# Experts' first product of a 1-core mixture block: weights as the stationary operand, gathered rows moving

## The reference, cut

```python
def swiglu_clamped(h):
    glu = jnp.minimum(h[..., ::2], SWIGLU_LIMIT)
    lin = jnp.clip(h[..., 1::2], -SWIGLU_LIMIT, SWIGLU_LIMIT)
    return glu * jax.nn.sigmoid(SWIGLU_ALPHA * glu) * (lin + 1.0)
...
    xs = xt[slot_tok].reshape(nb, MOE_BLOCK, D)

    def expert_block(args):
        xb, e = args
        hid = xb @ w1[e] + b1[e]
        return swiglu_clamped(hid) @ w2[e] + b2[e]

    ys = lax.map(expert_block, (xs, block_e)).reshape(P, D)
    out = jax.ops.segment_sum(ys.astype(jnp.float32) * slot_w[:, None], slot_tok, num_segments=T)
```

## Time and profile before

| | us |
|---|---|
| median of 3 runs | 3551.31 (3549.64 to 3569.22) |
| profiled execution | 3563.45 |
| its span | 3561.6 |
| mean granted TensorE clock in it | 0.933 |

### The profile page before, as it was taken

One profiled execution on the slowest core, in us unless ns is written; L12 is line 12 of the kernel. 1 busy time (PEld: TensorE's weight loads), 2 busy tenths in 40 slices (PEclk: granted clock), 3 DMA queues, 4 the chain that ended last, 5 costly groups with the idle time before them and its releaser, 6 DMA issues.

```text
span 3561.6 us, 42339 instructions
## 1 busy us (share of the span) xinstructions
PE 3276.9 (92%) x15738; PEld 2693.2 (76%) x15738; DVE 2349.4 (66%) x2341; ACT 1573.6 (44%) x1576; POOL 187.6 (5%) x212
## 2 busy tenths in 40 slices
PE   7967997999999988999999987769999999999995
PEld 6756986877778757878787765658888888888884
DVE  4545336457763556467754437459999999999995
ACT  2142214242223434332223215247777777777772
POOL 0000000000000000000000000001111111111110
PEclk9958978999999989999999996779999999999997
DMA  5200002334443302334433310259999999999993
GB/s 180 86 1 1 1 2 71 105 114 130 144 131 101 95 30 87 99 104 148 142 107 113 100 53 7 89 220 372 377 390 377 389 379 388 378 389 377 389 378 129
DMA packets 118820, 638.42 MB, mean 179 GB/s; under 512 B 13416, under 2 KB 13416, under 8 KB 68784
## 3 DMA queue, kind: packets, MB, share of 16 engines
q1 hardware_dynamic: 98592, 560.52, 42.5%
q0 software_dynamic: 20112, 76.24, 7.1%
HBM read 612.07 MB, written 24.64 MB: 179 GB/s over the span
## 4 chain that ended last, share of the span: by engine, by line
PE 74%; DVE 8%; ACT 1%; issue 1%; DMA 1%; DVEq 0%; SPq 0%; ACTq 0%; POOLq 0%
PE banks L328 25%; PE banks L2657 19%; PE banks L2674 10%; PE banks L1029 7%; PE banks L341 3%; DVE chunk_split L301 1%; PE banks L2651 1%; PE banks L2642 1%; PE banks L2663 1%; PE banks L547 1%; PE banks L570 1%; PE banks L1983 1%; DVE scratch L1127 0%; DVE scratch L389 0%; DVE scratch L1123 0%
## 5 line engine op out<-in xcount | busy, mean ns | idle before, releaser
L328 PE MATMUL banks<-x_scratch,chunk_split 128*128 128x512 f32 x3648 | 846.5, 393 | 36.4 <-DVE x_scratch L315 22.7
L328 PEld LDWEIGHTS banks<-x_scratch,chunk_split 128*128 128x128 f32 x3648 | 686.5, 189 | 190.1 <-issue 47.7
L295 ACT CAST chunk_split<-weight_ring 128x1024 fp32r<-128x1024 f32 x292 | 306.3, 1049 | 957.6 <-PE banks L328 721.0
L2657 PE MATMUL banks<-pair_split,rows 128*128 128x512 f32 x3072 | 709.9, 392 | 0.0
L2657 PEld LDWEIGHTS banks<-pair_split,rows 128*128 128x128 f32 x3072 | 578.6, 188 | 126.5
L301 DVE TENSOR_TENSOR chunk_split<-weight_ring,chunk_split 128x1024 fp32r<-128x1024 f32 x292 | 357.2, 1223 | 211.0 <-ACT chunk_split L295 202.4
L2674 PE MATMUL banks<-pair_split,hidden_t 128*128 128x512 f32 x1536 | 361.4, 394 | 6.1 <-DVE hidden_t L2769 6.1
L2674 PEld LDWEIGHTS banks<-pair_split,hidden_t 128*128 128x128 f32 x1536 | 285.5, 189 | 69.1 <-issue 6.3
L2436 DVE TENSOR_TENSOR pair_split<-mixed,pair_split 128x2048 fp32r<-128x2048 f32 x128 | 293.1, 2291 | 34.4 <-ACT pair_split L2431 34.4
L2436 DVE TENSOR_TENSOR pair_split<-scratch,pair_split 128x2048 fp32r<-128x2048 f32 x128 | 290.4, 2289 | 36.8 <-ACT pair_split L2431 36.8
L2436 DVE TENSOR_TENSOR pair_split<-weight_ring,pair_split 128x2048 fp32r<-128x2048 f32 x128 | 290.3, 2289 | 36.1 <-ACT pair_split L2431 36.1
(11 more groups left out here) (600 smaller groups left out, 3945.9 us busy)
## 6 DMA issues: line engine op xcount, KB each, us to landing
weight_ring<-in_weights SPq DMA_DIRECT2D x292, 512.0 KB, 3.7
mixed<-in_w SPq DMA_DIRECT2D x128, 1024.0 KB, 8.9
weight_ring<-in_w SPq DMA_DIRECT2D x128, 1024.0 KB, 7.8
scratch<-in_w SPq DMA_DIRECT2D x128, 1024.0 KB, 8.6
mixed<-in_w_ada POOLq DMA_DIRECT2D x48, 512.0 KB, 3.8
token_sums<-tables POOLq DMA_DIRECT2D x1, 2560.0 KB, 21.5
residual<-in_x POOLq DMA_DIRECT2D x4, 512.0 KB, 10.4
projected<-in_mem POOLq DMA_DIRECT2D x2, 1024.0 KB, 5.2
```

Source lines behind the costliest of these rows:

```text
L295: act.copy(chunk_split[:, 0, at:at + KB * P], flat(ring[:, n % RING])).then_inc(chunk_hi.sem, 1)
L328: mm = pe.matmul(lin.bank(j), chunk_split[:, a, at + k * P:at + (k + 1) * P], lin.split[b][k][:, 0:lin.tokens], start=(k, a, b) == (0, 0, ...
L2657: mm = pe.matmul(banks[:, n, :], rows[:, a, k, :], pair_split[k % SLOTS][:, b, n * T:(n + 1) * T], start=False, stop=(k, a) == (KB - 1, 1))
```

## The change

In the first product the operands trade places. The stationary operand is now a block of a pair, 128 input features x 128 output features, and the moving one a 128 x 128 block of the gathered rows. Sixteen blocks of each pair go to sixteen 128-column regions of banks 0 to 3, each with the three products, so output features lie on partitions and tokens along the banks. The columns of `w1` and `b1` are put apart on the host (all `glu`, then all `lin`), so banks 0 and 1 hold `glu`, 2 and 3 `lin`. The hidden block is then already in the layout of the second product: `turn_hidden` and its semaphores go, and `hidden_out` reads `lin` in SBUF. The bias has its rows on partitions 0 to 7 in another arrangement and becomes the stationary operand of its matmul, whose contraction is 8 rows. PE has a new wait for `lin_ready` ahead of each first product in the loop, since nothing else now says that the banks have been read.

```diff
-                dve.scalar_tensor_tensor(b1_pick[:, n, :], vec("part").to_broadcast([P, P]), float(32 + n),
+                dve.scalar_tensor_tensor(b1_pick[:, n, :], vec("part").to_broadcast([P, P]), float(4 + n),
...
                     pe.wait_ge(b1_copied, count)
+                    if not isinstance(count, int):
+                        pe.wait_ge(lin_ready, count + (-1))
                     for n in range(4):
-                        mm = pe.matmul(banks[:, n, :], b1_pick[:, n, :], b1_split, start=True, stop=False)
+                        mm = pe.matmul(banks[:, n, :], b1_split[0:8, n * P:(n + 1) * P],
+                                       b1_pick[0:8].rearrange("p n c -> p (n c)"), start=True, stop=False, skip_group_check=True)
                     mm.then_inc(b1_used, 1)
                     for k in range(PAIRS_IN):
                         pe.wait_ge(pair_lo, number + (k + 1))
-                        for a, b in PARTS:
-                            for n in range(4):
-                                mm = pe.matmul(banks[:, n, :], rows[:, a, k, :], pair_split[k % SLOTS][:, b, n * T:(n + 1) * T],
-                                               start=False, stop=(k, a) == (KB - 1, 1))
+                        for m in range(2 * KB):
+                            for a, b in PARTS:
+                                mm = pe.matmul(banks[:, m // 4, (m % 4) * P:(m % 4 + 1) * P],
+                                               pair_split[k % SLOTS][:, b, m * P:(m + 1) * P], rows[:, a, k, :],
+                                               start=False, stop=(k, a) == (KB - 1, 1), skip_group_check=True)
                         mm.then_inc(pair_used, 1)
-
-                def turn_hidden():
...
                 def hidden_out(count):
-                    act.wait_ge(hidden_turned, count)
-                    act.copy(hid_t[:, 0], banks[:, 6:8, :].rearrange("p b (k s) -> p (b k) s", s=P)).then_inc(hidden_hi, 1)
+                    act.wait_ge(hidden_ready, count)
+                    act.copy(hid_t[:, 0], lin.rearrange("p (k s) -> p k s", s=P)).then_inc(hidden_hi, 1)
...
-                    halves = banks[:, 0:4, :].rearrange("p b (f two) -> p b f two", two=2)
-                    dve.tensor_scalar(glu.rearrange("p (b f) -> p b f", b=4), halves[:, :, :, 0], 7.0, None, ALU.min)\
+                    dve.tensor_scalar(glu.rearrange("p (b f) -> p b f", b=2), banks[:, 0:2, :], 7.0, None, ALU.min)\
...
-                    sp.dma_start(b1_rows[32 * part:32 * part + 4, :], src.rearrange("a (n t) -> (a n) t", n=4))\
+                    sp.dma_start(b1_rows[4 * part:4 * part + 4, :].rearrange("q (n p) -> q n p", p=P),
+                                 src.rearrange("a (n q p) -> (a q) n p", n=4, q=4))\
                         .then_inc(b1_landed, 16)
```

More of the change, by code:

```diff
@@ L2400, in program @@
         b1_rows, b1_split = region(SCR_AT + 33 * T, T), rounded_tensor("b1_split", SCR_AT + 34 * T, T)
-        b1_turn, b1_stored, b1_zeroed = sem("b1_turn"), sem("b1_stored"), sem("b1_zeroed")
+        b1_turn, b1_stored = sem("b1_turn"), sem("b1_stored")
         b1_landed, b1_copied, b1_used = sem("b1_landed"), sem("b1_copied"), sem("b1_used")
@@ L2404, in program @@
         glu_ready, lin_ready, silu_out, hidden_ready = sem("glu_ready"), sem("lin_ready"), sem("silu_out"), sem("hidden_ready")
-        hidden_turned, hidden_hi, hidden_lo = sem("hidden_turned"), sem("hidden_hi"), sem("hidden_lo")
+        hidden_hi, hidden_lo = sem("hidden_hi"), sem("hidden_lo")
         y_ready, scattered, row_in_ready, row_out_ready, asked = sem("y_ready"), sem("scattered"), sem("row_in_ready"), sem("row_out_ready"), sem("asked")
@@ L2457, in store_tokens @@
         def store_tokens(pool):
-            pool.memset(b1_rows, 0.0).then_inc(b1_zeroed, 1)
             pool.wait_ge(b1_turn, 2)
@@ L2654, in first_product @@
                         pe.wait_ge(pair_lo, number + (k + 1))
-                        for a, b in PARTS:
-                            for n in range(4):
-                                mm = pe.matmul(banks[:, n, :], rows[:, a, k, :], pair_split[k % SLOTS][:, b, n * T:(n + 1) * T],
-                                               start=False, stop=(k, a) == (KB - 1, 1))
-                        mm.then_inc(pair_used, 1)
-                def turn_hidden():
[L2662 to L2665, removed]
+                        for m in range(2 * KB):
[3 more added lines that the diff above has]
+                                               start=False, stop=(k, a) == (KB - 1, 1), skip_group_check=True)
+                        mm.then_inc(pair_used, 1)
                 def second_product(number):
@@ L2681, in pe @@
                 turn_rows(2)
-                pe.wait_ge(hidden_ready, 1)
-                pe.wait_ge(rows_lo, 2)
-                turn_hidden()
                 last = last_item(pe)
@@ L2691, in pe @@
                     second_product(pair_number(i, PAIRS_IN))
-                    pe.wait_ge(hidden_ready, i + 2)
-                    pe.wait_ge(rows_lo, i + 3)
-                    turn_hidden()
                 pe.wait_ge(hidden_lo, last + 1)
@@ L2757, in hidden @@
                     dve.wait_ge(pair_used, used)
-                    halves = banks[:, 0:4, :].rearrange("p b (f two) -> p b f two", two=2)
-                    dve.tensor_scalar(glu.rearrange("p (b f) -> p b f", b=4), halves[:, :, :, 0], 7.0, None, ALU.min)\
+                    dve.tensor_scalar(glu.rearrange("p (b f) -> p b f", b=2), banks[:, 0:2, :], 7.0, None, ALU.min)\
                        .then_inc(glu_ready, 1)
-                    dve.tensor_scalar(lin.rearrange("p (b f) -> p b f", b=4), halves[:, :, :, 1], 7.0, -7.0, ALU.min, ALU.max)\
+                    dve.tensor_scalar(lin.rearrange("p (b f) -> p b f", b=2), banks[:, 2:4, :], 7.0, -7.0, ALU.min, ALU.max)\
                        .then_inc(lin_ready, 1)
@@ L2768, in hidden_out @@
                     dve.wait_ge(hidden_hi, count)
-                    dve.tensor_tensor(hid_t[:, 1], banks[:, 6:8, :].rearrange("p b (k s) -> p (b k) s", s=P), hid_t[:, 0],
+                    dve.tensor_tensor(hid_t[:, 1], lin.rearrange("p (k s) -> p k s", s=P), hid_t[:, 0],
                                       ALU.subtract).then_inc(hidden_lo, 1)
@@ L2864, in expert_loads @@
             sp.wait_ge(b1_stored, 32)
-            sp.wait_ge(b1_zeroed, 1)
             bias(0, 0)
@@ L3130, in _pack @@
     out["b_router"] = a["b_router_2"].reshape(1, E_N)
-    out["w1"], out["b1"] = a["w1_2"][0].reshape(E_N * KB, P, 2 * D), a["b1_2"][0].reshape(E_N * 4, T)
+    out["w1"] = a["w1_2"][0].reshape(E_N * KB, P, D, 2).transpose(0, 1, 3, 2).reshape(E_N * KB, P, 2 * D)
+    out["b1"] = a["b1_2"][0].reshape(E_N, D, 2).transpose(0, 2, 1).reshape(E_N * 4, T)
     out["w2"] = a["w2_2"][0].reshape(E_N * KB // 2, 2, P, D).transpose(0, 2, 1, 3).reshape(E_N * KB // 2, P, 2 * D)
```

## The result

The changed kernel takes 4790.71 us (median of 4 executions) against 3557.13 us for the kernel before, measured side by side: 1.344 times as long, 95% interval 1.337 to 1.352. The forecast was 4140 us. The sign was right; the size was not: +1234 us where +588 was forecast, less than half. The time lies in the stated range, between the forecast and the 5250 to 5440 us of rival B.

What follows compares the result with a forecast made beforehand. The prediction took PE, busy 92% of the span, to bound the kernel. First product +619, transposes -25, start and tail -6 made +588 us: 4151 on the profiled execution, 4140 against the median; range 4100 to 5500 us.

Steps and rivals of the forecast that it cites:

- rival B: First product: granted clock falls to 0.50 under the short matmuls, 213 ns each; 5250 to 5440 us; chance 0.25.
- The bound and the loads: PE alone sets the item's time; first product's 12,288 stationary loads, four times as many, set the pitch: +619 us.
- The load-record view: First product: summing load records, 12,288 at 188 ns, gives 2310 us, +1608; the prediction rejected it.
- C: First product: short moving operands stream like plain fp32, two records each, 232 ns; 5670 us; chance 0.10.
- E: First product: loads vanish beside the streaming, 57.2 ns a matmul; 3520 us; chance 0.03.
- D: First product: loads hide better, 66 ns pitch, 3630 us, or some 3815 at 81 ns; chance 0.12.
- what lies beside PE: Clamp, rounding, bias DMAs, GpSimd clearing and added wait: priced at nothing; 77 us if the cover failed.
- Rows 8: Trace rows: matmuls on 64 of 128 rows, read as back to back from 446.75; clock 1.00 at 451, 0.50 from 455.
- The pitch: First product: short matmuls 107.5 ns apart from start to start, +619 us; with 120 ns, +772 us.
- The start: First two items: PE's gap shrinks, -7 us; short matmuls at 1.2 GHz until the clock rises, +2 us.
- Rows 7: Trace rows: full 128x128 loads with 128 and 64 columns, 213 to 229 us, clock 0.50, 213 ns each.
- Transposes and tail: Hidden block's transposes go, 0.79 us x 32 = -25 us; wait before the last second product, perhaps -1 us.

Runs made afterwards that it cites:

- the kernel with the raised start: Changed kernel with 128-row bias, plus 24 unused 512-column matmuls ahead of the first two items' first products: 4195.08 us.

## Why the prediction was right or wrong

**The bound and the loads** were right: PE alone sets the item, loads are four times as many, and the pitch is that of a load, not of 128 columns. The load-record view would have given +1608 us for the loads alone; with the clock held, the kernel with the raised start pays +641 in all. Rivals C and E are out by the pitch, and so is D: at a granted clock of 1.00 the matmuls stand 111.8 ns apart, where D had 66. The Trainium skill, page "TensorE: Matmul & The Clock Gate", section "Back-to-back issue gap", has about 81 ns for sustained matmuls of 128 columns; for these fp32r operands it doesn't hold. Its section "LDWEIGHTS (loading the stationary operand)" has the columns over 1.2, which makes an estimate of 106.7 ns, near the measured value at the full clock and half of the 213.5 ns at the lower one.

**The step that failed** is the clock of the first product. The forecast priced all 12,288 short matmuls at the full clock and set rival B, the fall, apart as something for the whole loop; the trace has both, item by item. The sum had no term for what the change does to the four bias matmuls: the part on what lies beside PE speaks only of their DMAs, while the matmuls went from 128 rows to 8. The runs with the bias on 128 rows, left out, moved and doubled show that these tip the clock, where they stand between 512-column matmuls and short ones. Without that the changed kernel takes 4274.71 us instead of 4790.71: 516 us, for 13 items of 39 us and their second products.

**Rival B** had the price of an item's fall, 213 ns a matmul, but its cause only in part. It let the short matmuls bring the clock down because they leave the array idle for half of each load. With 128 columns they did not: behind full-height matmuls they kept 1.00 for 43 us in all 30 items. With 64 columns they did. Rows 8 were also misread. The half-height matmuls do not run back to back until the clock is down; PE first waits 0.67 us for VectorE, and the clock, 1.00 up to that wait, is 0.50 behind it:

```profile
454.48 3.97 PE L1640 MATMUL banks<-projected,scratch 64*128 64x128 f32 x16 [0.67 <-DVE scratch L1728]
```

So they hinted that matmuls on part of the rows do little for the clock, and did not show it. The prediction used them for the short matmuls, which use all rows, and not for the one group in the change that uses 8.

**The pitch was mis-sized** by 4.3 ns: 107.5 taken from the one-column rows, 111.8 measured, inside the bounds of 107.5 and 120. That is 12,288 x 4.3 ns = 53 us, 619 against 671.

**The start** had the right sign for the gap and not for the clock. PE's gap after the first item shrank from 12.01 us to 3.22, -8.8 where -7 was reckoned. But the clock was to rise within a few us of short matmuls, +2 us; it didn't rise at all in the first two items, 2 x 39 = 78 us. Rows 7 had shown just this, 16 us of short matmuls at 0.50. The three terms, 516 for the bias matmuls, 78 for the start and 53 for the pitch, make 647 of the 651 us between 4140 and 4791.

**Transposes and tail.** The 0.79 us a transposed block was right (the 128-row kernel with old operands is 30 us faster than before, for 26 forecast). The 8-row bias took 0.4 us of it back in every item, which no row had shown. The wait before the last second product did not shrink: 6.71 us for 6.06. `lin_ready` never held PE, and no copy came onto the path.

## What to carry to other kernels

Before swapping operands, count stationary loads, not columns: with 64 or 128 moving columns of fp32r data the load set the pace here, 112 ns for each 128x128 block at the full clock, and 256 columns came at 120 ns. Then ask of each stretch what clock it leaves for the next: load-bound matmuls of 128 columns lived on a clock that others had raised, and one microsecond of matmuls on 8 rows at the seam lost it for 80 us in 13 of 30 items. If such matmuls are needed, put them inside the dense stretch, or give them full height with zeros.

## What the runs showed of the hardware that was not expected

- The granted clock has a memory. The same 384 short matmuls, back to back, ran at 1.00 for 43 us or at 0.50 for 82 us, by what was ahead of them. The Trainium skill, page "TensorE: Matmul & The Clock Gate", section "Part 1: The HAM clock gate", says that "the default state is throttled, and activity releases the throttle"; the runs add that a PE with no idle time may not be active enough: 82 us of short matmuls didn't release it. Twenty-four 512-column ones ahead of them did, both times; eight did in one item of two.
- Matmuls on 8 rows count for little in this: 1.1 us of them between the dense and the short matmuls cost 13 of 30 items the full clock, 2.1 us all of them, 2.0 us on 128 rows none in the trace. Rows of zeros were enough for that.
- The number of moving columns counts too: behind the same full-height bias, short matmuls of 128 columns kept the clock in 30 items of 30, those of 64 columns, at the same pitch, in none.
- A load of a 128x128 fp32r block with a short matmul behind it takes 213.5 ns at 1.2 GHz, whether 64 or 128 columns follow (81.96 and 82.02 us for 384).
- With the old operands, an item whose four bias matmuls use 8 rows takes 0.46 us more than one where they use 128 (35.19 and 34.73 us), spread over the three steps around the seam. The origin of the 4 ns in the pitch at 2.4 GHz is open.
